# Index logits taken three per job from job 7 on, with seven top-k rounds and two low parts in other jobs, in a two-layer gated token-mixer trunk on Trainium2

## The chip, the core and the metric

The kernel runs on one core of one Trainium2 chip. The metric is the device time of one execution in microseconds (us).

## What is computed

A trunk of DEPTH = 2 layers on x of 512 tokens by 1024 channels, all in float32. Per layer, cut to what matters here:

```python
h = rms_norm(x, norm_g)
proj = h @ w_in       # a_u a_v a_z | q k v z_b | index queries, index key, head weights | g_a g_b
y_a = gelu(a_u) * spatial_gate(layer_norm(gelu(a_v))) * silu(a_z)
# sparse attention: the indexer picks the keys of every query
logits = einsum('bqhd,bsd->bqhs', qi, ki)                 # 8 index heads of 64
score  = einsum('bqh,bqhs->bqs', wi, relu(logits)) * idx_scale
idx    = top_k(where(admissible, score, -inf), 128)       # per query, shared by the 4 heads
y_b = attention(q, k[idx], v[idx]) * silu(b_z)
x = x + (sigmoid(g_a) * (y_a @ w_oa) + sigmoid(g_b) * (y_b @ w_ob)) @ w_out
```

## The kernel before

**Jobs.** TensorE (PE) works through 96 jobs per layer, numbered 0 to 95: four for the index queries (iq, 0 to 3), then k (4 to 7), q (8 to 11), v (12 to 25: v of branch B and v of branch A together), u (26 to 29), z_b (30 to 33), z_a (34 to 37), the gate g_a (38 to 51), w_oa (52 to 59), g_b (60 to 73), w_ob (74 to 81) and w_out (82 to 95). Each product runs in three passes, on a high and a low part of both operands. The groups of 14 jobs are seven half-size products with sums of blocks. A job of k, q, u, z_b or z_a is 24 matmuls of 512 columns, `three_pass`; a job of v or a gate is half of that.

**Engines.** Each engine has its own list of instructions, written out by one loop over the jobs. "Turn n" is what such a loop issues for job n. An engine takes its list strictly in order and waits at semaphores. In a turn VectorE (DVE) first makes low parts of weights (`remainder`, L1580, one 128 x 1024 subtraction per weight unit; which unit in which turn is in `quarters_in` and its tables, among them OB_UNITS); then it finishes the rope rotation of the job before (`rotated`, jobs 0 to 11); then layer norm, top-k rounds, and the job's own result (`evacuate`); last the side work (`beside`). Up to job 37 the rounds come before `evacuate`, from job 38 on after `beside`. ScalarE (ACT) makes the high parts of weights (L1181), copies results out of PSUM, and does the exponentials and the relu.

**Weights.** They come in units of 512 KB into a ring of four raw buffers (w_raw). The DMA of unit u waits for the low part of unit u-4 (s_wlo). Units of sums are added to the buffer's old content by a DMA that GpSimd (POOL, L763) issues. PE waits for the low part of a unit before the first job that uses it.

**Banks.** Results of k, q, u, z_b and z_a rotate through PSUM banks 0, 1, 2 (job number mod 3). The gate jobs take bank 0, 2, 1 or 6; job 38 takes bank 0, which job 36 had, and job 39 takes bank 1, which job 37 had. For z_a, `evacuate` on VectorE (L1791) multiplies ScalarE's tanh(z/2) plus 1 with z in the bank, and only then signals the bank free.

**Index logits.** IDX_STEPS are 24 steps: query blocks b = 1, 2, 3 (128 queries; a block sees 256, 384 or 512 keys), 8 heads each. Step i is two matmuls (L886, L887) into bank 3 + i % 2, a relu on ScalarE (L1427) into probs[i % 2], and a weighted add into score on VectorE (`index_add`, L1640 for the first head and L1642 for the others; after head 8 the mask, L1648). PE waits for relu i-2, relu i for add i-2. AFTER_IDX says after which job steps are taken: two after each of jobs 6 to 17.

**Top-k.** The 128 keys of a block are 16 rounds of MAX8 and MATCH_REPLACE8 (`topk_round`, L1653, L1654) over its whole score, and one closing pass (L1656). TOPK_SLOTS gives {job: [(block, rounds)]}.

**Attention.** 16 steps, block by block, of QK, row max (L1671), exponential (L1451), scaling (L1457), transposes on PE (L926), and the product with v (L917): step 0 after job 36, 1 after job 38, then after every second job; steps 8 to 11 (block 2) after jobs 52 to 58, 12 to 15 (block 3) from job 60 on. Transposes of step i are issued behind the next slot's job.

## Time and profile before

| | |
|---|---|
| median of 3 runs | 788.0 us (787.08 to 789.36) |
| the profiled execution | 789.16 us, span 786.5 us |
| mean granted TensorE clock | 0.998 of full |
| PE busy | 764.6 us (97%) |
| VectorE busy | 621.1 us (79%) |
| ScalarE busy | 447.1 us (57%) |

The profiled execution is 1.16 us above the median; 2.66 us of it lie outside the span. Layer 1 repeats layer 0 some 384 to 385 us later. PE's matmuls overlap, so that of a wait of PE the distance between starts counts: it is some 0.17 us more than the idle time that the rows show.

### The profile page before, as it was taken

The page shows a single profiled execution, that of the slowest core. Times are in us where ns is not written, and L with a number is a line of the kernel's source. Part 1 is how long each engine was busy: PE and PEld are TensorE (multiplying, and loading weights), DVE is VectorE, ACT ScalarE, POOL GpSimd, SP SyncE. Part 2 cuts the span into 40 slices and gives each one's busy share as a digit, 9 for nine tenths or more (in the row PEclk, how much of TensorE's full clock was granted, in tenths as well). Part 3 has the DMA queues.
Part 4 walks back from the last instruction along what each step waited for, and adds up shares of the span by engine and source line. Part 5 has one row for each costly group of instructions (what it writes and reads, how often), then busy time and mean ns, then how long its engine had stood idle before and what let it go on. Part 6 is the DMA issues. An engine that isn't in the chain of part 4 may idle for free.

```text
span 786.5 us, 12260 instructions
## 1 busy us (share of the span) xinstructions
PE 764.6 (97%) x4364; PEld 666.6 (85%) x4364; DVE 621.1 (79%) x1075; ACT 447.1 (57%) x834; POOL 153.3 (19%) x143
## 2 busy tenths in 40 slices
PE   7999999999999999999999999899999999999998
PEld 7988877888898879988899887688889987899886
DVE  5766899898878785779986679988988768756895
ACT  5588786341576437735665977564326763577242
POOL 1445430000130103012214453100012101110130
PEclk9999999999999999999999999999999999999999
DMA  9849998422695328685875888962348743486684
GB/s 333 274 94 201 188 196 260 137 77 70 195 169 183 73 63 142 206 237 105 194 232 156 180 164 173 266 212 81 107 75 215 167 135 53 94 151 223 176 144 125
DMA packets 60876, 128.34 MB, mean 163 GB/s; under 512 B 3984, under 2 KB 10320, under 8 KB 60816
## 3 DMA queue, kind: packets, MB, share of 16 engines
q0 software_dynamic: 26544, 55.66, 38.7%
q1 hardware_dynamic: 33984, 71.31, 27.6%
q8 instruction: 35, 0.57, 0.3%
q10 hardware_dynamic: 288, 0.59, 0.2%
q14 instruction: 25, 0.20, 0.1%
HBM read 107.63 MB, written 10.49 MB: 150 GB/s over the span
## 4 chain that ended last, share of the span: by engine, by line
PE 71%; DVE 14%; issue 7%; ACT 5%; DMA 3%; POOL 0%; DVEq 0%; ACTq 0%; POOLq 0%
PE bank L945 10%; PE bank L944 10%; PE bank L943 10%; PE bank L1012 6%; PE bank L1094 5%; PE bank L1014 5%; PE bank L1013 5%; DVE score L1654 2%; DVE w_lo L1580 2%; DVE top L1653 2%; PE bank L1041 2%; PE bank L980 2%; PE bank L1042 2%; PE bank L1043 2%; PE bank L982 2%
## 5 line engine op out<-in xcount | busy, mean ns | idle before, releaser
L1580 DVE TENSOR_TENSOR w_lo<-w_raw,w_hi 128x1024 fp32r<-128x1024 f32 x168 | 203.2, 1219 | 31.9 <-ACT w_hi L1181 27.6
L1181 ACT ACTIVATE w_hi<-w_raw 128x1024 fp32r<-128x1024 f32 x168 | 173.1, 1053 | 36.7 <-DMA w_raw<-in_w_out 14.7
L763 POOL DMA_DIRECT2D w_raw<-in_w_in x48 | 59.1, 1231 | 374.1 <-DVE w_lo L1580 374.1
L1012 PE MATMUL bank<-h_hi,w_lo 128*128 128x256 f32 x256 | 76.5, 299 | 3.5 <-DVEq L1761 3.5
L943 PE MATMUL bank<-h_lo,w_hi 128*128 128x512 f32 x192 | 75.2, 392 | 0.0
L945 PE MATMUL bank<-h_hi,w_hi 128*128 128x512 f32 x192 | 74.7, 389 | 0.0
L944 PE MATMUL bank<-h_hi,w_lo 128*128 128x512 f32 x192 | 74.7, 389 | 0.0
L1014 PE MATMUL bank<-h_hi,w_hi 128*128 128x256 f32 x256 | 73.2, 286 | 0.0
L1013 PE MATMUL bank<-h_lo,w_hi 128*128 128x256 f32 x256 | 73.1, 286 | 0.0
L1451 ACT ACTIVATE probs<-probs,neg_max,rstd 128x128 f32<-128x128 f32 (+3 forms) x32 | 20.9, 654 | 69.8 <-DVE neg_max L1675 69.7
L1653 DVE MAX8 top<-score 128x8 f32<-128x256 f32 (+2 forms) x96 | 53.5, 557 | 5.0 <-DVE g_a L1802 1.9
L1012 PE MATMUL bank<-hs,w_lo 128*128 128x256 f32 x192 | 56.3, 293 | 0.0
L1012 PEld LDWEIGHTS bank<-h_hi,w_lo 128*128 128x128 f32 x256 | 49.8, 195 | 5.5 <-DVEq L1761 3.9
L1014 PE MATMUL bank<-hs,w_hi 128*128 128x256 f32 x192 | 53.8, 280 | 0.0
L1013 PE MATMUL bank<-hs,w_hi 128*128 128x256 f32 x192 | 53.8, 280 | 0.0
L1654 DVE MATCH_REPLACE8 score<-top,score 128x256 f32<-128x256 f32 (+2 forms) x96 | 52.1, 543 | 0.0
L1013 PEld LDWEIGHTS bank<-h_lo,w_hi 128*128 128x128 f32 x256 | 49.7, 194 | 1.6 <-issue 1.4
L943 PE MATMUL bank<-w_lo,h_hi 128*128 128x512 f32 x128 | 50.4, 394 | 0.0
L945 PE MATMUL bank<-w_hi,h_hi 128*128 128x512 f32 x128 | 50.1, 391 | 0.0
L944 PE MATMUL bank<-w_hi,h_lo 128*128 128x512 f32 x128 | 49.9, 390 | 0.0
L1014 PEld LDWEIGHTS bank<-h_hi,w_hi 128*128 128x128 f32 x256 | 49.7, 194 | 0.0
L945 PEld LDWEIGHTS bank<-h_hi,w_hi 128*128 128x128 f32 x192 | 36.0, 188 | 7.5
(234 smaller groups left out, 1986.0 us busy)
## 6 DMA issues: line engine op xcount, KB each, us to landing
w_raw<-in_w_in SPq DMA_DIRECT2D x84, 512.0 KB, 4.6
w_raw<-in_w_in POOLq DMA_DIRECT2D x48, 512.0 KB, 6.1
w_raw<-in_w_out POOLq DMA_DIRECT2D x16, 512.0 KB, 6.6
w_raw<-in_w_out SPq DMA_DIRECT2D x12, 512.0 KB, 4.2
out<-x_sb POOLq DMA_DIRECT2D x4, 1024.0 KB, 5.8
w_raw<-in_w_oa SPq DMA_DIRECT2D x8, 512.0 KB, 3.4
w_raw<-in_w_ob SPq DMA_DIRECT2D x8, 512.0 KB, 4.4
x_sb<-out POOLq DMA_DIRECT2D x2, 2048.0 KB, 10.6
```

The costliest lines, as they stand in the source:

```text
L763: pool.dma_start(w_raw[:, slot], block_weights(layer, u), accum_op=ALU.add) \
L943: nc.tensor.matmul(dst, s_h, m_l, start=(n == 0), stop=False)
L944: nc.tensor.matmul(dst, s_l, m_h, start=False, stop=False)
L945: last = nc.tensor.matmul(dst, s_h, m_h, start=False, stop=(n == len(pairs) - 1))
L1012: nc.tensor.matmul(dst, w_lo[:, wk, col], a_hi[:, k], start=first and i == 0, stop=False, skip_group_check=True)
L1013: nc.tensor.matmul(dst, w_hi[:, wk, col], a_lo[:, k], start=False, stop=False, skip_group_check=True)
L1014: last = nc.tensor.matmul(dst, w_hi[:, wk, col], a_hi[:, k], start=False, stop=(k == HALF_K - 1), skip_group_check=True)
L1094: last = nc.tensor.matmul(dst[:, 0:width], h[:, k, tok], w[:, k, first:first + width], start=(k == 0 and n == 0), stop=(k == KD - 1 and n ...
L1181: nc.scalar.activation(hi, w_raw[:, raw_slot(layer, u)], ACT.Copy).then_inc(s_whi.sem, 1)
L1580: nc.vector.tensor_tensor(lo, w_raw[:, raw_slot(layer, u)], hi.bitcast(F32), ALU.subtract) \
L1653: vec.link(dve, nc.vector.max(top8[:], s))
L1654: vec.link(dve, nc.vector.match_replace(s, top8[:], s, TAKEN))
```

## The change

1. **Index logits.** Steps 0 and 1 stay behind job 6. For each of the jobs 7 to 11 there is now one step in the middle (MID_IDX: 2, 5, 8, 11, 14: PE issues it after the fourth of the eight k of the job) and two steps behind it (3, 4; 6, 7; 9, 10; 12, 13; 15, 16). Two each follow jobs 12, 13, 14 and one (23) job 15. ScalarE takes the relu of the middle step ahead of its `evacuate`, VectorE the add ahead of the rounds and of `evacuate`.
2. **Top-k rounds.** By job, as rounds before and after: 9: 0, 1; 10: 3, 2; 11: 3, 1; 27: 3, 4; 28: 3, 4; 31: 1, 2; 34: 0, 1; 35: 0, 1; 46: 1, 0; 47: 1, 0; 45: 1, 2; 49: 1, 0; 50: 0, 1; 55: 2, 1; 57: 1, 0; 58: 0, 1; 59: 1, 0. Job 37 has two rounds of block 3 where it had two of block 2, job 39 one of block 3 where it had one of block 2. Block 1 closes in turn 28 (27 before), block 2 in 35 (39), block 3 in 58 (59).
3. **Low parts.** In OB_UNITS VectorE's second unit of the next group is made in turn +11 where it was in +10: turns 23, 49 and 71 for 22, 48 and 70.

z keeps its tanh on ScalarE and its product on VectorE. The diff:

```diff
--- before.py
+++ after.py
@@ -110,7 +110,7 @@
 
 GATE_UNITS = dict(scalar=[0, 1, 3, 5], vector=[1, 2, 5, 7])
 LATE_GATE_UNITS = dict(scalar=[0, 0, 2, 2, 3, 4, 6, 7, 8, 8], vector=[0, 1, 2, 3, 4, 5, 7, 7, 8, 9])
-OB_UNITS = dict(scalar=[9, 9, 10, 11], vector=[10, 10, 11, 12])
+OB_UNITS = dict(scalar=[9, 9, 10, 11], vector=[10, 11, 11, 12])
 LATE_UNITS = dict(scalar=[-1, 0, 1, 1, 4, 5, 6, 7, 9, 9], vector=[-1, 1, 2, 3, 5, 6, 7, 8, 9, 10])
 
 
@@ -182,7 +182,10 @@
 AFTER_K = {JOB_K[t] + 2: t for t in range(TILES)}
 AFTER_Q = {JOB_Q[t] + 2: t for t in range(TILES)}
 IDX_STEPS = [(b, h) for b in range(1, TILES) for h in range(IH)]
-AFTER_IDX = {6 + n // 2: [n - n % 2, n - n % 2 + 1] for n in range(len(IDX_STEPS))}
+MID_IDX = {JOB_K[3] + i: 2 + 3 * i for i in range(5)}
+AFTER_IDX = {JOB_K[2]: [0, 1], **{n: [i + 1, i + 2] for n, i in MID_IDX.items()},
+             **{JOB_V[i]: [17 + 2 * i, 18 + 2 * i] for i in range(3)}, JOB_V[3]: [23]}
+assert sorted([*MID_IDX.values(), *(i for steps in AFTER_IDX.values() for i in steps)]) == list(range(len(IDX_STEPS)))
 AFTER_WS = JOB_V[8]
 LN_TILES = {JOB_ZB[0]: [0, 1], JOB_ZB[1]: [2, 3]}
 AFTER_MIX = {JOB_ZB[3]: [0, 1], JOB_ZA[0]: [2, 3]}
@@ -206,10 +209,10 @@
 
 VA_DONE = {JOB_V[9]: 0, JOB_V[10]: 1, JOB_V[11]: 2, JOB_V[12]: 3}
 
-TOPK_SLOTS = {10: [(1, 3)], 11: [(1, 3)], 19: [(1, 1)], 20: [(1, 1)], 21: [(1, 1)], 26: [(1, 4)], 27: [(1, 3)],
-              28: [(2, 3)], 29: [(2, 4)], 30: [(2, 1)], 31: [(2, 1)], 32: [(2, 2)], 33: [(2, 2)], 37: [(2, 2)], 39: [(2, 1)],
-              **{n: [(3, 1)] for n in range(41, 53, 2)}, 46: [(3, 1)], 52: [(3, 1)], 53: [(3, 2)],
-              54: [(3, 1)], 55: [(3, 2)], 56: [(3, 1)], 57: [(3, 1)], 59: [(3, 1)]}
+TOPK_SLOTS = {9: [(1, 1)], 10: [(1, 2)], 11: [(1, 1)], 19: [(1, 1)], 20: [(1, 1)], 21: [(1, 1)], 26: [(1, 4)], 27: [(1, 4)],
+              28: [(1, 1), (2, 3)], 29: [(2, 4)], 30: [(2, 1)], **{n: [(2, 2)] for n in range(31, 34)}, 34: [(2, 1)], 35: [(2, 1)],
+              37: [(3, 2)], 39: [(3, 1)], 41: [(3, 1)], 43: [(3, 1)], 45: [(3, 2)], 50: [(3, 1)], 51: [(3, 1)], 52: [(3, 1)],
+              53: [(3, 2)], 54: [(3, 1)], 55: [(3, 1)], 56: [(3, 1)], 58: [(3, 1)]}
 
 
 
@@ -1078,6 +1081,8 @@
                     def ready(k):
                         if j == 0 and k % 2 == 0:
                             pe.wait_ge(s_wlo.sem, s_wlo.at(layer, UNIT_FIRST[g] + k // 2 + 1))
+                        if k == HALF_K and n in MID_IDX:
+                            index_logits(layer, MID_IDX[n])
                 last = three_pass(dst[:], pairs, ready)
                 last.then_inc(s_job.sem, 1)
 
@@ -1415,16 +1420,19 @@
                         act_.join(act)
                         act.sem_inc(s_rotc.sem, 1)
 
+            def index_relu(layer, i):
+                b, h = IDX_STEPS[i]
+                w = P * (b + 1)
+                act.wait_ge(s_idxp.sem, s_idxp.at(layer, i + 1))
+
+                if i >= 2:
+                    act.wait_ge(s_idx.sem, s_idx.at(layer, i - 1))
+                nc.scalar.activation(probs[:, i % 2, 0:w], bank[3 + i % 2][:, 0:w], ACT.Relu).then_inc(s_relu.sem, 1)
+
             def beside(layer, n):
 
                 for i in AFTER_IDX.get(n, []):
-                    b, h = IDX_STEPS[i]
-                    w = P * (b + 1)
-                    act.wait_ge(s_idxp.sem, s_idxp.at(layer, i + 1))
-
-                    if i >= 2:
-                        act.wait_ge(s_idx.sem, s_idx.at(layer, i - 1))
-                    nc.scalar.activation(probs[:, i % 2, 0:w], bank[3 + i % 2][:, 0:w], ACT.Relu).then_inc(s_relu.sem, 1)
+                    index_relu(layer, i)
                 if n == AFTER_WS:
                     act.wait_ge(s_wst.sem, s_wst.at(layer, 1))
                     four = bank[5][:].rearrange("p (c q) -> p c q", c=A_GROUPS)
@@ -1535,6 +1543,8 @@
                         rounded(layer, u)
                     if AFTER_QI.get(n) == 0:
                         rotated_copied(layer, n)
+                    if n in MID_IDX:
+                        index_relu(layer, MID_IDX[n])
                     evacuate(layer, n)
                     if AFTER_QI.get(n) != 0:
                         rotated_copied(layer, n)
@@ -1975,6 +1985,8 @@
                             small_remainder(layer + 1)
                             remainder(layer + 1, 2)
                     layer_norm(layer, n)
+                    if n in MID_IDX:
+                        index_add(layer, MID_IDX[n])
                     if n < JOB_GA[0]:
                         topk(n)
                     evacuate(layer, n)
```

The three places where the order on VectorE decides. First, turn 11 behind its rotation, and turn 12 up to its own (the last q job and the first v job; rot is the rotated q that PE transposes). Before:

```order
L1653 MAX top<-score 128x8
L1654 MATCH_REPLACE score<-top,score 128x256
L1653 MAX top<-score 128x8
L1654 MATCH_REPLACE score<-top,score 128x256
L1653 MAX top<-score 128x8
L1654 MATCH_REPLACE score<-top,score 128x256
L1778 RECIPROCAL rstd<-std 128x4
L1642 SCALAR_TENSOR_TENSOR score<-probs,head_w,score 128x384 x2
L1580 TENSOR_TENSOR w_lo<-w_raw,w_hi 128x1024
L1590 SCALAR_TENSOR_TENSOR rope_b<-stage,rope_g 128x4x64
L1591 TENSOR_TENSOR rope_b<-stage,rope_g 128x4x64
L1594 TENSOR_TENSOR rot<-rope_a,rope_b 128x512
```

and now:

```order
L1652 SCALAR_TENSOR_TENSOR score<-probs,head_w,score 128x384
L1663 MAX top<-score 128x8
L1664 MATCH_REPLACE score<-top,score 128x256
L1788 RECIPROCAL rstd<-std 128x4
L1652 SCALAR_TENSOR_TENSOR score<-probs,head_w,score 128x384
L1658 TENSOR_TENSOR score<-score,diag 128x128
L1650 TENSOR_SCALAR score<-probs,head_w 128x512
L1590 TENSOR_TENSOR w_lo<-w_raw,w_hi 128x1024
L1600 SCALAR_TENSOR_TENSOR rope_b<-stage,rope_g 128x4x64
L1601 TENSOR_TENSOR rope_b<-stage,rope_g 128x4x64
L1604 TENSOR_TENSOR rot<-rope_a,rope_b 128x512
```

Two of the three rounds are gone. In place of two adds of 384 columns stand two of 384, a mask and a first add of 512 columns; the low part and the rotation of turn 12 follow as before.

Second, turn 37 (the last z_a job; the first row belongs to attention step 0 in turn 36, the last is the product that frees bank 1 for job 39). Before:

```order
L1661 RECIPROCAL row_inv<-row_sum 128x1
L1653 MAX top<-score 128x8
L1654 MATCH_REPLACE score<-top,score 128x384
L1653 MAX top<-score 128x8
L1654 MATCH_REPLACE score<-top,score 128x384
L1791 SCALAR_TENSOR_TENSOR silu_um<-t_half,bank 128x512
```

and now:

```order
L1671 RECIPROCAL row_inv<-row_sum 128x1
L1663 MAX top<-score 128x8
L1664 MATCH_REPLACE score<-top,score 128x512
L1663 MAX top<-score 128x8
L1664 MATCH_REPLACE score<-top,score 128x512
L1801 SCALAR_TENSOR_TENSOR silu_um<-t_half,bank 128x512
```

The two rounds ahead of the product run over 512 columns where they ran over 384. Two turns earlier, in turn 35, a round and the closing pass of block 2 now stand ahead of that turn's product, and in turn 34 a round.

Third, turns 46 (from its last attention row on), 47 and 48 (g_a; of the rows with g_a<-g_a,bank the last one is the add that PE's job 50 waits for). Before:

```order
L1661 RECIPROCAL row_inv<-row_sum 128x1
L1653 MAX top<-score 128x8
L1654 MATCH_REPLACE score<-top,score 128x512
L1580 TENSOR_TENSOR w_lo<-w_raw,w_hi 128x1024
L1760 TENSOR_TENSOR g_a<-g_a,bank 128x2x256
L1653 MAX top<-score 128x8
L1654 MATCH_REPLACE score<-top,score 128x512
L1580 TENSOR_TENSOR w_lo<-w_raw,w_hi 128x1024 x2
L1760 TENSOR_TENSOR g_a<-g_a,bank 128x2x256
```

and now:

```order
L1671 RECIPROCAL row_inv<-row_sum 128x1
L1590 TENSOR_TENSOR w_lo<-w_raw,w_hi 128x1024
L1770 TENSOR_TENSOR g_a<-g_a,bank 128x2x256
L1590 TENSOR_TENSOR w_lo<-w_raw,w_hi 128x1024
L1770 TENSOR_TENSOR g_a<-g_a,bank 128x2x256
```

The rounds of turns 46 and 47 and one of two low parts are gone from ahead of turn 48's add. One round was put into turn 45.

## Rows read from the trace of the kernel before

**Rows 1.** The page: busy time; shares of the chain that ended last.

```profile
PE 764.6 (97%) x4364; PEld 666.6 (85%) x4364; DVE 621.1 (79%) x1075; ACT 447.1 (57%) x834; POOL 153.3 (19%) x143
...
PE 71%; DVE 14%; issue 7%; ACT 5%; DMA 3%; POOL 0%; DVEq 0%; ACTq 0%; POOLq 0%
```

**Rows 2.** Waits of PE, layer 0, 57 to 130 us: total, times, longest.

```profile
PE bank L1041 <- DVE w_lo L1580: 1.3, 1, 1.3
PE bank L872 <- DVE rot L1594: 1.2, 1, 1.2
```

**Rows 3.** The same view, layer 1, 441 to 516 us.

```profile
PE bank L886 <- ACT probs L1427: 0.8, 1, 0.8
```

**Rows 4.** The same view, layer 0, 240 to 300 us.

```profile
PE bank L926 <- ACT probs L1457: 1.4, 2, 1.0
```

**Rows 5.** VectorE by form: count, busy us, mean ns, idle before.

```profile
L1653 DVE MAX8 top<-score 128x8 f32<-128x512 f32 x32 | 22.0, 688 | 3.3 <-DVE g_a L1802 1.9 <-DVE g_a L1760 0.9
L1654 DVE MATCH_REPLACE8 score<-top,score 128x512 f32<-128x512 f32 x32 | 21.6, 676 | 0.0
...
L1653 DVE MAX8 top<-score 128x8 f32<-128x384 f32 x32 | 17.8, 557 | 1.1 <-DVE z_b L1784 0.5
L1654 DVE MATCH_REPLACE8 score<-top,score 128x384 f32<-128x384 f32 x32 | 17.4, 543 | 0.0
L1653 DVE MAX8 top<-score 128x8 f32<-128x256 f32 x32 | 13.6, 425 | 0.6
...
L1642 DVE SCALAR_TENSOR_TENSOR score<-probs,head_w,score 128x512 f32<-128x512 f32 x14 | 10.5, 751 | 1.9 <-ACT probs L1427 1.0 <-DVE v_b L1735 0.5
...
L1654 DVE MATCH_VALUE_LOAD score<-top,score 128x8 f32 x96 | 8.8, 92 | 3.3
L1642 DVE SCALAR_TENSOR_TENSOR score<-probs,head_w,score 128x384 f32<-128x384 f32 x14 | 8.6, 613 | 0.3
...
L1656 DVE TENSOR_SCALAR score<-score 128x384 f32<-128x384 f32 x2 | 0.7, 361 | 0.1
```

**Rows 6.** PE in order of time: index steps 8 and 9, to job 11.

```profile
83.68 0.42 PE L886 MATMUL bank<-ki_lo,qi_t 128*128 128x384 f32 x1
...
84.47 0.39 PE L943 MATMUL bank<-w_lo,h_hi 128*128 128x512 f32 x1
```

**Rows 7.** VectorE in order of time, turns 11 and 17: start, us.

```profile
90.65 0.43 DVE L1590 SCALAR_TENSOR_TENSOR rope_b<-stage,rope_g 128x256 f32<-128x256 f32 x1 [0.89 <-PE bank L872]
...
116.94 1.22 DVE L1580 TENSOR_TENSOR w_lo<-w_raw,w_hi 128x1024 fp32r<-128x1024 f32 x1
```

**Rows 8.** The same view, turns 28, 30, 36 and 37.

```profile
152.84 2.36 DVE L1580 TENSOR_TENSOR w_lo<-w_raw,w_hi 128x1024 fp32r<-128x1024 f32 x2 [1.06 <-ACT w_hi L1181]
...
165.31 0.18 DVE L1847 RECIPROCAL ln_rstd<-ln_std 128x4 f32<-128x4 f32 x1 [0.22 <-ACT ln_std L1209]
...
204.00 0.69 DVE L1791 SCALAR_TENSOR_TENSOR silu_um<-t_half,bank 128x512 f32<-128x512 f32 x1 [0.70 <-ACT t_half L1380]
...
207.63 0.16 DVE L1661 RECIPROCAL row_inv<-row_sum 128x1 f32<-128x1 f32 x1 [0.70 <-ACTq L1455]
...
210.19 0.69 DVE L1791 SCALAR_TENSOR_TENSOR silu_um<-t_half,bank 128x512 f32<-128x512 f32 x1
```

**Rows 9.** PE in order of time: the first matmul of job 39.

```profile
212.01 0.36 PE L1012 MATMUL bank<-h_hi,w_lo 128*128 128x256 f32 x1
```

**Rows 10.** PE in order of time, layer 0: the first matmul of job 50.

```profile
249.48 0.39 PE L1012 MATMUL bank<-h_hi,w_lo 128*128 128x256 f32 x1 [1.73 <-DVEq L1761]
```

**Rows 11.** The same in layer 1: job 50.

```profile
634.32 0.39 PE L1012 MATMUL bank<-h_hi,w_lo 128*128 128x256 f32 x1 [1.74 <-DVEq L1761]
```

**Rows 12.** A window behind it: busy times, then granted clock, DMA share, GB/s.

```profile
634.60:638.10 3.50, 3.50 (x19) 3.50 (x19) 2.51 (x7) 2.64 (x6) 0.00 (x0) 0.51 0.71 248
```

**Rows 13.** PE in order of time: scores of attention step 8, layers 0 and 1.

```profile
259.84 0.49 PE L935 MATMUL bank<-k_t,q_t 128*128 128x384 f32 x1
...
646.15 0.49 PE L935 MATMUL bank<-k_t,q_t 128*128 128x384 f32 x1
```

## Prediction

> **What bounds the kernel now.** I read the page first: PE is busy for 97% of the span, and the chain that ended last runs over PE for 71% and over VectorE for 14% [rows 1]. So there is no second bound of any length, only places where PE waits, and a gain has to be one of these waits. The views of PE's waits give them. In the v stage of layer 0 PE waits twice: 1.2 us for the rotation of the last q tile, 1.3 us for a weight low part [rows 2]. Layer 1 adds 0.8 us in which an index matmul waits for a relu [rows 3]. In the g_a stage job 50 waits 1.73 us for VectorE's add of turn 48 [rows 10]; in the w_oa and g_b stages two transposes of probabilities wait 1.4 us in all [rows 4]. Every one goes back to VectorE being late. With the tails of the matmuls (0.17 us per wait) the two later groups cost 1.9 and 1.7 us in each layer. The question for each part is therefore what VectorE has to do before a given instruction, and whether PE stands waiting for it.
>
> There is a second loss in layer 1. After the same wait as in layer 0 [rows 10, 11] the granted clock falls to 0.51 for 3.5 us [rows 12], that is, to 1.2 GHz of 2.4. Between job 50's first matmul and the scores of attention step 8, layer 0 takes 259.84 - 249.48 = 10.36 us, layer 1 takes 646.15 - 634.32 = 11.83 us [rows 10, 11, 13]: the fall cost 1.5 us.
>
> **Prices.** A top-k round is MAX8, the load and MATCH_REPLACE8: 0.688 + 0.092 + 0.676 = 1.46 us over 512 columns, 0.557 + 0.092 + 0.543 = 1.19 over 384, and about 0.425 + 0.092 + 0.41 = 0.93 over 256 (the replace taken as long as the MAX8, as in the other widths). An index add is 0.75 us (512) or 0.61 (384), a closing pass 0.36 (384) [rows 5]. On PE two steps of 384 columns take 84.47 - 83.68 = 0.79 us, 0.4 each [rows 6].
>
> **Index logits and the v stage.** No step is added, so PE's own time stays. Five more steps (10 to 14, 384 columns) are issued before job 11 ends: PE is 5 x 0.4 = 2.0 us later there, and VectorE's turn 11, which waits for the transposes behind job 11 (the 0.89 us ahead of it [rows 7]), starts 2.0 us later. From there to the low part at 116.94 VectorE works without a pause. In this stretch two rounds of 256 are gone (-1.9), four adds of 384 (-2.5) make room for two of 512 (+1.5) and a mask (0.3 us, taken like the closing pass): -2.6. Net the low part that PE waits for comes 0.6 us earlier. The wait for the rotation vanishes, but its 1.2 us come back as a longer wait at that low part. Layer 1 has the same 0.6 and the relu's 0.8, because no relu stands behind a late weight any more. Together **-2.0 us**. It could be nothing (VectorE late by what it gained), or all the waits of rows 2 and 3 with their tails, 6.7 us for both layers.
>
> The middle steps are new waits: PE's step i stands in mid job, with all the job's matmuls queued behind it, and needs relu i-2. ScalarE comes to that relu only behind its squares, root and copies for the job before, PE to mid job behind four transposes, two steps and twelve matmuls: by the two lists about a tie for jobs 7 and 9, and room for the others. No row shows such a wait; the nearest are 0 and the 0.8 of rows 3. I take 0.15 us per layer, nearest to the tie, **+0.3**.
>
> **Rounds into z_b and z_a.** This is the part that costs. In turn 28 VectorE starts at 152.84 behind an idle 1.06 us, waiting for a high part that ScalarE can make only behind job 27 [rows 8]; that idle time swallows turn 27's extra round. From there to the product of turn 37 at 210.19 there is added: one round of 256 (0.93) and the closing pass of block 1 (0.3), rounds of 384 in turns 31, 34 and 35 (3.57), the closing pass of block 2 (0.36), and in turn 37 two rounds of 1.46 for two of 1.19 (0.54): 5.7, with the few hundredths between instructions 5.8 us. The waits that this can fill are 0.22 us (turn 30) and 0.70 us (turn 36, tanh of job 36). The other 0.70, the exponential of attention step 0, is a round trip that stays [rows 8]. So the product that frees bank 1 ends 4.9 us later, at 215.8 instead of 210.88. PE began job 39, which needs that bank, at 212.01 [rows 9], 0.1 us of which is the signal's way: 1.0 us of slack. PE waits **3.9 us in each layer, +7.8**, in which the late scaling of step 0's probabilities (4 us later too) is contained. VectorE then stays 1 us behind PE until turn 44, so that banks 2 and 6 come back just in time; I count nothing, at most 0.5 us per layer.
>
> **Rounds out of g_a and w_oa, the low part.** Ahead of the add of turn 48 two rounds leave (turns 46 and 47), one arrives (turn 45), and one low part leaves: -1.46 - 1.22 = -2.7 us, more than the wait of 1.9. It goes in both layers: **-3.8**. The moved low part falls into turn 49, ahead of the add for job 51, but behind a turn that starts 2.7 us earlier: hidden; without that cover it would cost its 1.2. In turns 22 and 70 nothing waits: 0. For the transposes behind job 58 PE needs step 10's maximum (turn 56): by then two rounds in all are gone (-2.9), while PE comes 1.9 earlier; so 1.0 us of the first wait (the longest, 1.0 plus its tail [rows 4]) goes. By step 11 it is a third round, and the second wait goes whole. **-3.3** for both layers. The DMAs hang on the low parts: in z_a they start up to 5 us later, but the high parts made from them are a group away.
>
> **Sum** without the clock: -2.0 + 0.3 + 7.8 - 3.8 - 3.3 = -1.0 us. **The clock.** Waits of 1.73 us were followed by a fall once in two layers [rows 10 to 12]. Now these waits are gone (-1.5), but a wait of 3 us and one of half a microsecond stand around job 38 in each layer, longer than the one that brought the fall. I take a fall in both layers: 3.4 us at half clock, +1.7 each, +3.4. Total 789.16 - 1.0 - 1.5 + 3.4 = 790.1 us for the profiled execution; the median of the runs lies 1.16 us below that execution, which gives **788.9 us**.
>
> **Rivals.**
> 1. *The clock stays full behind the new wait.* For it: in layer 0 the 1.73 us did not bring a fall. Against it: layer 1, and the new wait is twice as long. 785.5 us. The Trainium skill (TensorE: Matmul & The Clock Gate, "HAM oscillation") lets only idle gaps longer than these waits, and than the one forecast here, cost the clock; by that rule this rival would be the forecast, but this trace shows a fall behind 1.74 us of idle time, so it does not agree. Chance 0.16.
> 2. *VectorE takes the rounds in its stride in z_b and z_a*, because its 79% leave room and the waits there are longer than I read. Then +7.8 and +3.4 fall away: 777.7 us. Against it: between 152.84 and 210.19 only 0.92 us of idle time can be filled. Chance 0.10.
> 3. *Slower: the clock also falls in the v stage.* PE now reaches job 18 without an earlier wait and meets a VectorE that is late with two low parts in succession: the 2.8 us that rows 2 give with their tails, less the 0.6 gained, are 2.2 us of waiting with six matmuls between. If such a pair brings the clock down, which a single 1.3 did not, both layers pay 1.7 us more: 792.3 us. [...] Chance 0.26.
>
> **Numbers.** The forecast has 0.48. 0.3% is 2.4 us, about what a measurement of this kernel can tell from no change: below 785.6 is faster, above 790.4 slower. Faster is rival 2, more than half of rival 1 and a little of the forecast: 0.24. Slower is rival 3: 0.26. Same: 0.50. The range runs from 784.9 (rival 1 and a v stage that gains a little more) to 792.6 (rival 3 with the 0.5 us of the banks) and leaves rival 2 out.
>
> **What would show it.** Right: in the view of PE's waits job 39 waits 3 to 4 us for the signal behind VectorE's silu_um product, in both layers; the wait before job 50 and those of the transposes behind jobs 58 and 60 are gone; the wait for the rotation is gone, two for w_lo in job 18 remain; the granted clock falls behind job 39's wait. Wrong: no wait at job 39 (then rival 2), or waits in mid job at L886's successor of more than 0.5 us, which would mean that the relus are late and that the v stage starts later than I think.

## The result and the profile after

| | before | after |
|---|---|---|
| median, range | 787.58 us (787.08 to 789.36, 4 runs) | 797.8 us (795.81 to 799.12, 4 runs) |
| profiled execution | 789.16 us, span 786.5 us | 797.21 us, span 794.6 us |
| mean granted clock | 0.998 | 0.994 |

The ratio is 1.0114, with a 95% interval of 1.0093 to 1.0134: the change makes the kernel 10 us **slower**. I had forecast 788.9 us, no change, in a range up to 792.6. The profiled executions differ by 8.05 us, the medians by 10.2, because before the median lies 1.6 us under the profiled execution (1.16 by the three runs that the forecast knew) and after the change 0.6 us above it.

The page of the changed kernel, busy times and the chain that ended last, which answers to [rows 1]:

```profile
PE 768.6 (97%) x4364; PEld 669.1 (84%) x4364; DVE 618.9 (78%) x1075; ACT 448.7 (56%) x834; POOL 154.0 (19%) x143
...
PE 57%; DVE 25%; ACT 7%; issue 6%; DMA 5%; DVEq 0%; ACTq 0%; SPq 0%
```

VectorE does no more than before, yet its share of the chain has grown from 14 to 25%, and that of the DMA from 3 to 5%. (Lines from L886 of before are 3 to 10 higher now: L1580 is L1590, L1012 is L1015, L1760 is L1770, L1041 is L1044.)

Waits of PE after the change (total, times, longest), layer 0 in four stretches: 57 to 130, 130 to 146, 204 to 265, 265 to 300 us. They answer to [rows 2, 4]:

```profile
PE bank L1044 <- DVEq L1748: 1.4, 1, 1.4
PE bank L1044 <- DVE w_lo L1590: 0.3, 1, 0.3
PE bank L875 <- DVEq L1642: 0.3, 1, 0.3
PE bank L889 <- ACT probs L1430: 0.2, 1, 0.2
...
PE bank L1044 <- DVEq L1746: 3.4, 2, 2.5
...
PE bank L1015 <- DVEq L1803: 2.7, 1, 2.7
PE bank L1015 <- DVEq L1771: 0.8, 1, 0.8
PE bank L929 <- ACT probs L1465: 0.3, 1, 0.3
...
PE bank L920 <- DVE z_b L1890: 0.2, 1, 0.2
```

The wait for the rotation is gone, and so is the old wait before job 50. In job 18 0.3 us are left of the wait for the low part; 1.4 us stand in job 17 now, for a bank that the add of turn 15 frees. So VectorE's lateness comes back one job earlier than forecast, and at another instruction. Two waits are new and large: 3.4 us for the adds of turns 22 and 23 (2.5 in job 24 and 0.9 in job 25, where before PE lost 0.3 us at most), and 2.7 us in job 39. A third, 0.8 us, is in job 51.

To place each microsecond I took the end of each job's last matmul from the trace, and from it how long each group of jobs takes. In us, layer 0 / layer 1, against the terms of the prediction for both layers:

| jobs | before | after | difference, both | predicted |
|---|---|---|---|---|
| start to 23 | 134.14 / 120.70 | 133.32 / 119.56 | -2.0 | -2.0 + 0.3 |
| 24, 25 | 5.76 / 5.44 | 9.45 / 7.93 | **+6.2** | 0 |
| 26 to 37 | 69.15 / 69.15 | 69.15 / 69.15 | 0 | 0 |
| 38, 39 | 6.08 / 6.07 | 11.08 / 12.16 | +11.1 | +7.8 + 3.4 |
| 40 to 49 | 32.62 / 32.62 | 32.54 / 32.39 | -0.3 | 0 |
| 50 | 4.87 / 6.36 | 2.88 / 2.88 | -5.5 | -3.8 - 1.5 |
| 51 | 3.97 / 3.96 | 5.04 / 5.04 | **+2.2** | 0 |
| 52 to 61 | 37.79 / 37.81 | 36.37 / 36.03 | -3.2 | -3.3 |
| 62 to 95 | 104.21 / 102.67 | 103.83 / 102.67 | -0.4 | 0 |

The rows for which I had worked out a term are right to 0.3 us. The two set to nothing are 8.3 us; against the sum of 790.1 the profiled execution is 7.1 us longer, the other rows together being 1.2 us better than forecast.

**Job 39.** PE in order of time, layer 0, with the idle time ahead in brackets:

```profile
214.71 0.28 PE L1017 MATMUL bank<-h_hi,w_hi 128*128 128x256 f32 x1
215.34 0.33 PE L929 MATMUL bank<-eye,probs 128*128 128x128 f32 x1 [0.34 <-ACT probs L1465]
215.50 0.39 PE L938 MATMUL bank<-k_t,q_t 128*128 128x128 f32 x2
218.58 0.39 PE L1015 MATMUL bank<-h_hi,w_lo 128*128 128x256 f32 x1 [2.69 <-DVEq L1803]
```

VectorE in the same time:

```profile
214.76 0.68 DVE L1663 MAX8 top<-score 128x8 f32<-128x512 f32 x1
...
217.07 0.68 DVE L1664 MATCH_REPLACE8 score<-top,score 128x512 f32<-128x512 f32 x1
217.78 0.69 DVE L1801 SCALAR_TENSOR_TENSOR silu_um<-t_half,bank 128x512 f32<-128x512 f32 x1
```

The two rounds of turn 37 run from 214.76 to 217.75, and the product that frees bank 1 starts behind them. The clock falls to half in both layers: in layer 0 1.35 us after the wait has ended, in layer 1 already within it (job 39's first matmul starts at 606.96 there), and for 6.8 us (two windows; columns as in [rows 12]):

```profile
219.90:223.40 3.50, 3.50 (x19) 3.50 (x18) 2.77 (x8) 1.04 (x5) 1.20 (x1) 0.51 0.79 294
605.60:612.50 6.90, 5.54 (x26) 5.54 (x27) 5.74 (x11) 3.24 (x9) 1.20 (x1) 0.51 0.55 170
```

Here an idle time of 2.69 us, with 0.34 us shortly ahead, cost the clock in both layers, as 1.74 us did once in [rows 11, 12]. The Trainium skill (TensorE: Matmul & The Clock Gate, "HAM oscillation") has only longer idle gaps than this cost the clock; this trace does not agree.

The same wait need not bring a fall. In experiment 6, layer 1, job 39 waits as long and the clock stays full:

```profile
635.18 0.39 PE L1015 MATMUL bank<-h_hi,w_lo 128*128 128x256 f32 x1 [2.69 <-DVEq L1803]
...
633.00:640.00 7.00, 4.82 (x40) 4.83 (x41) 5.80 (x13) 3.71 (x8) 1.20 (x1) 1.00 0.63 223
```

Jobs 38 and 39 take 9.80 us there, 3.7 more than before the change: that is the wait alone. What the changed kernel takes beyond it, 1.3 us in layer 0 and 2.4 us in layer 1, is the clock.

**Jobs 24 and 25.** ScalarE in order of time, after the change:

```profile
125.30 1.06 ACT L1186 ACTIVATE w_hi<-w_raw 128x1024 fp32r<-128x1024 f32 x1 [2.86 <-DMA w_raw<-in_w_in]
129.29 1.06 ACT L1186 ACTIVATE w_hi<-w_raw 128x1024 fp32r<-128x1024 f32 x1 [2.93 <-DMA w_raw<-in_w_in]
130.37 1.28 ACT L1282 ACT_TABLE_LOAD   x1
...
132.83 2.00 ACT L1186 ACTIVATE w_hi<-w_raw 128x1024 fp32r<-128x1024 f32 x2 [0.17 <-ACT ws_t L1440]
```

and VectorE:

```profile
133.92 1.23 DVE L1590 TENSOR_TENSOR w_lo<-w_raw,w_hi 128x1024 fp32r<-128x1024 f32 x1 [0.73 <-ACT w_hi L1186]
135.06 0.68 DVE L1745 TENSOR_TENSOR v_a<-v_a,bank 128x512 f32<-128x512 f32 x1
...
136.72 2.33 DVE L1590 TENSOR_TENSOR w_lo<-w_raw,w_hi 128x1024 fp32r<-128x1024 f32 x2
138.96 0.68 DVE L1745 TENSOR_TENSOR v_a<-v_a,bank 128x512 f32<-128x512 f32 x1
```

Read it backwards. Job 24 waits for the add at 135.06; that stands behind a low part, that behind a high part at 132.83, that behind the table load and two copies, and these behind the high part at 129.29, which waited for **the last weight transfer of v to land**. Before the change the same high part ran at 126.37:

```profile
126.37 1.06 ACT L1181 ACTIVATE w_hi<-w_raw 128x1024 fp32r<-128x1024 f32 x1 [2.12 <-DMA w_raw<-in_w_in]
```

So ScalarE waited for landings in the v stage before the change too; the prediction does not read that view. The transfer itself (tile w_raw, POOL's queue, the last v transfer: issued at 118.5 us before, at 117.6 after), first before, then after:

```profile
DMA to landing us min/median/max: 7.9/7.9/7.9
```

```profile
DMA to landing us min/median/max: 11.7/11.7/11.7
```

It starts 0.9 us earlier and lands 2.9 us later. What it shares the DMA engines with has moved. SyncE's first two weight transfers of the next group, u, start at 119.97 and 122.12 us (122.36 and 123.49 before), because the low parts that give back their buffers come earlier. The v transfer ahead of it is issued 2.2 us earlier than it, where it was 4.0 us. And SyncE's two copies of hs (the high and the low part of a sum of blocks of h, 512 KB each, written to the DRAM buffer `hold`) run beside it for 3.9 and 6.7 us, before for 3.8 and 5.0. SyncE's queue after the change, 119.5 to 122.5 us:

```profile
L688 SPq DMA_DIRECT2D w_raw<-in_w_in x2: 384/384/384, 120.0 to 122.1; - x2
...
DMA to landing us min/median/max: 8.1/8.2/8.3
```

Two windows of each kernel (busy times, granted clock, DMA share, GB/s) show DMA engines that were never free, before as after (in a share above 1 the packets of an engine overlap); first before, then after:

```profile
116.00:120.00 4.00, 2.65 (x12) 1.85 (x11) 3.90 (x6) 2.12 (x5) 1.21 (x1) 1.00 1.11 216
120.00:124.00 4.00, 4.00 (x19) 3.23 (x18) 3.97 (x6) 2.75 (x4) 0.00 (x0) 1.00 1.05 302
```

```profile
116.00:120.00 4.00, 3.73 (x16) 2.71 (x15) 3.74 (x4) 3.52 (x6) 1.85 (x2) 1.00 1.10 268
120.00:124.00 4.00, 4.00 (x19) 3.22 (x18) 2.05 (x4) 1.43 (x2) 0.00 (x0) 1.00 1.10 271
```

From job 11's end to job 23's end PE became 3.0 us faster in layer 0 (44.03 to 41.05) and 3.8 us in layer 1; from job 11's end to the last v landing it is 36.2 and 36.7 us before, 37.0 and 35.4 after. So in layer 0 the stream of weights came later, in layer 1 earlier but by less than PE did. PE ran ahead of its weights and gave the lead back in jobs 24 and 25. That was the theory to test.

### The profile page after: what moved, and what is told of

Same layout as the page of the kernel before. It is cut to its first block, busy times and chain, and to the rows that moved or that the text cites. A ratio compares the mean times of both kernels' runs of the same rounds, so it can differ in the third digit from the quotient of the medians.

```text
span 794.6 us, 12256 instructions
## 1 busy us (share of the span) xinstructions
PE 768.6 (97%) x4364; PEld 669.1 (84%) x4364; DVE 618.9 (78%) x1075; ACT 448.7 (56%) x834; POOL 154.0 (19%) x143
## 4 chain that ended last, share of the span: by engine, by line
PE 57%; DVE 25%; ACT 7%; issue 6%; DMA 5%; DVEq 0%; ACTq 0%; SPq 0%
PE bank L948 7%; PE bank L947 7%; PE bank L946 7%; DVE w_lo L1590 6%; PE bank L1015 5%; PE bank L1016 5%; PE bank L1017 5%; PE bank L1099 4%; DVE score L1664 4%; DMA w_raw<-in_w_in 4%; DVE top L1663 4%; PE bank L983 3%; PE bank L984 3%; PE bank L985 3%; ACT w_hi L1186 2%
## 5 line engine op out<-in xcount | busy, mean ns | idle before, releaser
L1590 DVE TENSOR_TENSOR w_lo<-w_raw,w_hi 128x1024 fp32r<-128x1024 f32 x168 | 203.4, 1220 | 42.3 <-ACT w_hi L1186 36.8
L1015 PE MATMUL bank<-h_hi,w_lo 128*128 128x256 f32 x256 | 77.6, 303 | 7.0 <-DVEq L1803 5.4
L1015 PEld LDWEIGHTS bank<-h_hi,w_lo 128*128 128x128 f32 x256 | 50.9, 199 | 10.4 <-DVEq L1803 6.5
L1015 PE MATMUL bank<-hs,w_lo 128*128 128x256 f32 x192 | 56.1, 292 | 0.0
```

The source lines that it names most:

```text
L1015: nc.tensor.matmul(dst, w_lo[:, wk, col], a_hi[:, k], start=first and i == 0, stop=False, skip_group_check=True)
L1590: nc.vector.tensor_tensor(lo, w_raw[:, raw_slot(layer, u)], hi.bitcast(F32), ALU.subtract) \
```

## The experiments

Ratios are to runs of the kernel before on the same chip, whose median was 789.58 us for the first four, 790.5 for the next four, 790.28 for the ninth to twelfth and 788.84 for the last; for the change the ratio is 1.0114. A ratio is not the quotient of the two medians and can differ from it by 0.15%. Times of jobs are those of the profiled execution, one for each kernel.

**1. Index part alone.** The tables TOPK_SLOTS and OB_UNITS as before, the rest as in the change.

```diff
-OB_UNITS = dict(scalar=[9, 9, 10, 11], vector=[10, 11, 11, 12])
+OB_UNITS = dict(scalar=[9, 9, 10, 11], vector=[10, 10, 11, 12])
...
-TOPK_SLOTS = {9: [(1, 1)], 10: [(1, 2)], 11: [(1, 1)], 19: [(1, 1)], 20: [(1, 1)], 21: [(1, 1)], 26: [(1, 4)], 27: [(1, 4)],
+TOPK_SLOTS = {10: [(1, 3)], 11: [(1, 3)], 19: [(1, 1)], 20: [(1, 1)], 21: [(1, 1)], 26: [(1, 4)], 27: [(1, 3)],
...
```

> The index logits go three per job as in the change; all top-k rounds and the two low parts are where they were before. Theory A: the loss in the v stage belongs to the index part alone. The change's products end 3.1 us later than before at the end of job 25 in layer 0 and 1.4 us in layer 1, out of waits of 2.7 and 1.0 us (layer 0) and 1.2 and 1.0 us (layer 1) before jobs 24 and 25; they stay, and job 39's wait and the clock falls behind it are not there, while the old wait before job 50 is. That gives about 787.6 + 4.5 = 792. Rival B: those waits come from the rounds that went from jobs 10 and 11 to 9 and 27, the index part gains the 2 us that I predicted: 785.6.

794.79 us, ratio 1.006 (1.0038 to 1.0083), 5.2 us above before: A. Waits of PE, layer 0, 99 to 140 us:

```profile
PE bank L875 <- DVE rot L1604: 2.0, 1, 2.0
PE bank L1044 <- DVEq L1746: 1.7, 1, 1.7
PE bank L1044 <- DVEq L1748: 1.4, 1, 1.4
PE bank L1044 <- DVE w_lo L1590: 0.3, 1, 0.3
```

Job 24 waits; job 25 does not (2.79 us). With all six rounds in turns 10 and 11 the rotation is awaited 2.0 us where it was 1.2, so that the wait vanishes in the change only by the two rounds that leave: jobs 14 to 18 take 20.90 us here and 18.60 in the change. Jobs 38 and 39 are as before (6.07 us). By jobs, the index part alone has lost 2.2 us by the end of job 23 (both layers together), and 3.8 us more in job 24.

**2. Rounds of blocks 2 and 3 back.**

```diff
-              28: [(1, 1), (2, 3)], 29: [(2, 4)], 30: [(2, 1)], **{n: [(2, 2)] for n in range(31, 34)}, 34: [(2, 1)], 35: [(2, 1)],
-              37: [(3, 2)], 39: [(3, 1)], 41: [(3, 1)], 43: [(3, 1)], 45: [(3, 2)], 50: [(3, 1)], 51: [(3, 1)], 52: [(3, 1)],
-              53: [(3, 2)], 54: [(3, 1)], 55: [(3, 1)], 56: [(3, 1)], 58: [(3, 1)]}
+              28: [(1, 1), (2, 3)], 29: [(2, 4)], 30: [(2, 1)], 31: [(2, 1)], 32: [(2, 2)], 33: [(2, 2)], 37: [(2, 2)], 39: [(2, 1)],
+              **{n: [(3, 1)] for n in range(41, 53, 2)}, 46: [(3, 1)], 52: [(3, 1)], 53: [(3, 2)],
+              54: [(3, 1)], 55: [(3, 2)], 56: [(3, 1)], 57: [(3, 1)], 59: [(3, 1)]}
```

> The change with the rounds of blocks 2 and 3 (jobs 28 to 59) back where they were before; the index part, block 1's rounds and the low parts as in the change. Theory A: TensorE's 2.85 us wait in job 39 goes in both layers, and the clock falls behind it too (11.1 us in all), but the waits in job 50 (1.9 us a layer, with the clock's fall in layer 1) and before the transposes after jobs 58 and 60 come back (6.5 us in all): 797.8 - 11.1 + 6.5 = 793.2. Rival B: the wait in job 39 comes of everything in that layer standing later behind the v stage, not of the rounds: it stays, and the time is above 797.8.

790.8 us, ratio 1.0009 (0.9997 to 1.0021): A in kind, and 4 us better than I expected: 2 us are this chip's own time of the kernel before, the rest for the most part the clock, which stays full behind jobs 50 and 51. Job 39 takes 3.20 us in both layers, as before the change. Jobs 50 and 51 take 3.74 + 4.75 us instead of 4.87 + 3.97: the low part in turn 49 shifts part of the wait from job 50 to 51.

**3. Turn 37's rounds into turns 43 and 49.**

```diff
-              37: [(3, 2)], 39: [(3, 1)], 41: [(3, 1)], 43: [(3, 1)], 45: [(3, 2)], 50: [(3, 1)], 51: [(3, 1)], 52: [(3, 1)],
+              39: [(3, 1)], 41: [(3, 1)], 43: [(3, 2)], 45: [(3, 2)], 49: [(3, 1)], 50: [(3, 1)], 51: [(3, 1)], 52: [(3, 1)],
```

> The change with the two rounds of block 3 in VectorE's turn 37 put into turns 43 and 49. Theory A: they stand 2.98 us ahead of the product of job 37 that gives bank 1 back to job 39, so TensorE's 2.85 us wait there goes, and with it the clock falls at 219.9 and 605.6 us: 11.1 us less, given back at most 1 us by the two rounds' new places, so 787 (786 to 789). Rival B: the product is late for another reason (the rounds in turns 34 and 35, ScalarE's tanh): job 39 still waits 1 to 3 us in each layer, and the time stays above 791.

794.3 us, ratio 1.0063 (1.0041 to 1.0085): my number is wrong by 7, by 5 against its before. PE in order of time, job 39 and job 44 in layer 0, then VectorE's product of turn 37:

```profile
215.75 0.39 PE L1015 MATMUL bank<-h_hi,w_lo 128*128 128x256 f32 x1 [0.71 <-DVEq L1803]
...
233.81 0.39 PE L1015 MATMUL bank<-hs,w_lo 128*128 128x256 f32 x1 [0.71 <-DVE w_lo L1590]
...
214.94 0.69 DVE L1801 SCALAR_TENSOR_TENSOR silu_um<-t_half,bank 128x512 f32<-128x512 f32 x1 [0.95 <-ACT t_half L1385]
```

The clock stays full in both layers, and jobs 38 and 39 take 7.8 us instead of 11.1 and 12.2: 7.6 us are back. But 0.7 us of the wait stays although turn 37 has no round at all. VectorE has nothing to do ahead of that product: it stands idle for 0.95 us until ScalarE's tanh of job 37, which is issued behind the exponential and the scaling of attention step 0, and these waited for VectorE's row maximum. So what moved into turns 28 to 35 (four rounds and closing passes) makes that chain late enough for a wait, and the two rounds of turn 37 had hidden the chain's last 0.95 us. And the two rounds cost 5.2 us in their new places, not 1: jobs 40 to 49 are 1.0 and 1.5 us longer, job 51 0.3 in each layer, jobs 57 to 61 1.0 in each.

**4. u's weights only behind v's last landing.**

```diff
                         sp.wait_ge(s_wlo.sem, s_wlo.at(layer, u - RAW + 1))
+                    if u == UNIT_FIRST[V_G + 1]:
+                        sp.wait_ge(*landed(layer, u - 1))
                     slot = raw_slot(layer, u)
```

> The change, and SyncE's queue starts the first weight transfer of u only when the last added transfer of v has landed. Theory A: in the change the two u transfers start at 119.97 and 122.12 us (before: 122.36 and 123.49) because the low parts come earlier, share the DMA engines with the last two transfers of v, and make the last one land at 129.27 instead of 126.35; VectorE's add of job 22 follows from that landing, and job 24 waits for it. Held back, the last v transfer lands near 127 in layer 0, the waits before jobs 24 and 25 lose 2 to 3.7 us in layer 0 and 1 to 2.5 in layer 1: 793 (791.6 to 794.8). Rival B: the transfers of v are late by themselves (later starts at 103 us and a full DMA), the landing stays near 129 and the u weights come later yet: 797.8 or more.

794.57 us, ratio 1.006 (1.004 to 1.008): A. It is 5.0 us above its before, where the change is 10.2 above; between the two profiles it is 3.2 us. The same transfer as above, issued at 117.8 us:

```profile
DMA to landing us min/median/max: 9.3/9.3/9.3
```

It lands at 127.1 us (11.7 and 10.1 us for the transfer in the two layers of the change, 9.3 and 8.8 here). Job 24 takes 3.33 and 3.08 us instead of 5.56 and 4.03, job 25 an unchanged 3.90. So a second thing makes job 25 wait.

**5. The low parts back.**

```diff
-OB_UNITS = dict(scalar=[9, 9, 10, 11], vector=[10, 11, 11, 12])
+OB_UNITS = dict(scalar=[9, 9, 10, 11], vector=[10, 10, 11, 12])
```

> The change with the two low parts back in VectorE's turns 22 and 48 (and 70); index logits and rounds as in the change. Theory A: the low part that now stands in turn 23 ahead of the add of turn 23 is what job 25 waits for (1.03 us with its tail in each layer), and the one in turn 49 is what job 51 waits for (0.97 us). Both waits go; ahead of the adds of turns 22 and 48 it costs less, since in turn 22 VectorE sits idle for a high part anyway and in turn 48 there is 1.0 us of slack: -2.3 us in the v stage of both layers together, -2.1 us in job 51, +0.5 us in job 50, so 794. Rival B: it is the same work one turn earlier, and the waits only move to jobs 24 and 50, at their full 1.2 us: 797.5 to 798.

800.16 us, ratio 1.011 (1.0073 to 1.0147): against A, and no better than the change. Jobs 25 and 51 do lose their waits (3.07 and 2.75; 3.97 us), and job 50 pays 0.5 us in each layer, as expected. But in turn 22 the low part costs more than it saves: job 24 waits 3.9 us, and 2.6 in layer 1,

```profile
PE bank L1044 <- DVEq L1746: 3.9, 1, 3.9
```

and the clock falls with that in both layers, here in layer 0:

```profile
136.80:143.60 6.80, 6.10 (x14) 4.84 (x15) 5.95 (x10) 2.58 (x6) 0.00 (x0) 0.50 0.77 233
```

Job 24 takes 9.40 and 7.20 us. That is rival B for job 24. Inside the changed kernel the moved low part was a relief of turn 22, paid for in turn 23.

**6. The third index step behind the job.**

```diff
-MID_IDX = {JOB_K[3] + i: 2 + 3 * i for i in range(5)}
-AFTER_IDX = {JOB_K[2]: [0, 1], **{n: [i + 1, i + 2] for n, i in MID_IDX.items()},
+MID_IDX = {}
+AFTER_IDX = {JOB_K[2]: [0, 1], **{JOB_K[3] + i: [2 + 3 * i, 3 + 3 * i, 4 + 3 * i] for i in range(5)},
```

> The change with the third index step of jobs 7 to 11 behind the job, with the two others, instead of in mid job. Theory A: the third step then needs the relu of the first, which ScalarE does only behind the copy of the job's result, so that TensorE waits about 0.8 us at each of five places in each layer: 806. Rival B: TensorE has room there, since VectorE sets the pace of the v stage, and a wait in jobs 7 to 11 only takes the place of the 1.5 us wait in job 18: 798 to 800.

825.66 us, ratio 1.0449 (1.0411 to 1.0488). A, but three times my price: the five waits are 1.9 to 2.6 us each where I took 0.8, and the clock falls four times among them. PE's waits, layer 0, 57 to 150 us:

```profile
PE bank L889 <- ACT probs L1430: 11.8, 5, 2.6
```

A relu behind the job comes only after ScalarE's squares, root and copies for that job (64.76 to 66.80 us for the first of the five). The middle step is what makes three per job possible: in the change it costs PE 0.2 and 0.4 us of waiting in the two layers.

**7. The second and fourth together, v's low part back in turn 22.** The v group alone gets its own table, used for g == V_G:

```diff
+V_UNITS = dict(scalar=[9, 9, 10, 11], vector=[10, 10, 11, 12])
```

> The kernel of the second experiment (rounds of blocks 2 and 3 back), with the wait of the fourth experiment (u's first weight transfer only when v's last has landed), and in the v stage alone the low part back in turn 22. Theory A: the waits before jobs 24 and 25 go almost whole (jobs 24 and 25 took 8.95 us in layer 0 and 7.96 in layer 1 in the second experiment, 5.76 and 5.44 before): 790.8 - 5.7 = 785.1, faster than before. Rival B: with the low part back in turn 22, the add of turn 22 is late again by its 1.2 us in each layer, or the later u weights make job 26 wait: 787.5 to 789.

789.74 us, ratio 0.9991 (0.9973 to 1.0009): B. Job 24 takes 5.21 and 4.51 us, job 25 2.72 and 2.77. With u's weights held back, the high parts for the two low parts in turn 22 are late: ScalarE waits for their landings and makes them at 131.29 and 132.63 us, VectorE's two low parts take from 132.39 to 134.95, and the add that job 24 waits for stands behind them.

**8. The fourth's wait in the kernel before.**

> The kernel before, with nothing but the wait of the fourth experiment: u's first weight transfer only when v's last has landed. Theory A: before the change the last v transfer landed in time and jobs 24 and 25 hardly waited (0.28 us in layer 0), so the wait gives nothing: within 0.5 us of before. Rival B: the wait helps by itself, whatever the index logits do, and the fourth experiment says nothing about the change: 1.5 us or more below before.

789.86 us, ratio 0.9992 (0.9975 to 1.0009): A. In its profile the wait even costs job 24 1.1 and 0.6 us. The last v transfer gains nothing there by having u's out of its way (8.7 and 8.0 us, 7.9 and 7.5 in the kernel before). The traffic of u was no loss before; the index part made it one.

**9. One low part a turn further.**

```diff
-OB_UNITS = dict(scalar=[9, 9, 10, 11], vector=[10, 11, 11, 12])
+OB_UNITS = dict(scalar=[9, 9, 10, 11], vector=[10, 11, 12, 12])
```

> The change with one low part of each group moved one VectorE turn further: from turn 23 to 24, 49 to 50 and 71 to 72 (vector=[10, 11, 12, 12]). Theory A: job 25 waits for the add of turn 23, which stands behind two low parts; behind one it comes 1.2 us earlier, and so for job 51 and turn 49. Both waits go in both layers: 1.13 + 1.18 + 1.07 + 1.08 = 4.5 us less than the change, so 5.7 us above before instead of 10.2. Rival B: the low part is only passed on: job 26 or the transposes of the attention step behind job 50 wait for it, and the time stays within 1.5 us of the change.

794.71 us, ratio 1.0071 (1.0046 to 1.0095), 4.4 us above before by the medians and 5.6 by the ratio: A by the time. Job 25 takes 2.72 and 2.79 us, job 51 3.97: both waits are gone. But jobs 57 to 61 take 0.55 us more in each layer than in the change, where a product of attention waits: half of what job 51 gains is lost there again. In layer 0 its job 24 waits longer than in the change and the clock falls with it (7.43 us instead of 5.56).

**10. All three together.** The rounds of the second, the wait of the fourth, the low parts of the ninth; their diffs, one on the other.

> The second experiment (rounds of blocks 2 and 3 where they were before) with the wait of the fourth and the low parts of the ninth. Theory A: from job 11's end to job 25's the v stage is set by the stream of its weights. With u's transfers held back it ran in 48.2 and 48.0 us (before: 49.8 and 50.3, the change 50.5 and 49.0), with job 25's wait of 1.0 us still in it; without that 47.2 and 47.0. Against the second experiment that is 2.7 + 2.2 us, and 1.6 us in job 51: its 1.2 us above before become 5.3 us below before. Rival B: the three do not add up, because held back u weights are late for the low part in turn 22: at most 2 us below before.

785.45 us, ratio 0.9944 (0.9924 to 0.9965): 4.8 us below its before, A. PE's waits, layer 0, 120 to 260 us:

```profile
PE bank L1046 <- DVEq L1748: 1.2, 1, 1.2
PE bank L1017 <- DVEq L1773: 0.6, 1, 0.6
```

**11. SyncE's two copies of hs to `hold` kept back too.**

```diff
+                    if u == UNIT_FIRST[V_G + 1]:
+                        sp.wait_ge(*landed(layer, u - 1))
                     if u in (UNIT_FIRST[V_G] + 8, UNIT_FIRST[V_G + 1]):
```

> The tenth kernel, and the two copies of hs to hold are held back as well until v's last weight transfer has landed. Theory A: the last two v transfers share the DMA engines with these two copies (they start 24 us behind job 11's end, in the same 10 us); without them the last one lands at about 32 us behind job 11's end instead of 34.6 (fourth experiment), and what is left of job 24's wait (0.5 us in layer 0) goes: 0.5 to 1 us below the tenth kernel. Rival B: the copies cost the v transfers nothing: landing and time as in the tenth.

785.29 us, ratio 0.9943 (0.9926 to 0.9961). The last v transfer now takes

```profile
DMA to landing us min/median/max: 6.5/6.5/6.5
```

against 11.7, 31.8 us behind job 11's end, and job 24 does not wait (3.00 and 2.89 us). That is A's mechanism; the medians of 10 and 11 can't be told apart, their spans are 783.6 and 781.6 us. By jobs, from the second experiment to this one, the held back transfers give 3.3 us (jobs 12 to 24) and the later low part some 2.9 (jobs 25 and 51, less what jobs 52 to 61 give back). The copies were not held back with the change's own rounds.

**12. One round from turn 55 forward.**

```diff
-              28: [(1, 1), (2, 3)], 29: [(2, 4)], 30: [(2, 1)], 31: [(2, 1)], 32: [(2, 2)], 33: [(2, 2)], 37: [(2, 2)], 39: [(2, 1)],
+              28: [(1, 1), (2, 3)], 29: [(2, 4)], 30: [(2, 1)], 31: [(2, 2)], 32: [(2, 2)], 33: [(2, 2)], 37: [(2, 2)], 39: [(3, 1)],
...
-              54: [(3, 1)], 55: [(3, 2)], 56: [(3, 1)], 57: [(3, 1)], 59: [(3, 1)]}
+              54: [(3, 1)], 55: [(3, 1)], 56: [(3, 1)], 57: [(3, 1)], 59: [(3, 1)]}
```

> The tenth kernel with one round taken out of turn 55: a round of block 2 goes from turn 39 to turn 31, one of block 3 from 55 to 39. Theory A: the transposes behind jobs 58 and 60 lose their waits of 1.13 and 0.6 us in each layer (3.4 us); turn 37's product is 1.2 us later against 1.0 us of slack, at most 0.3 us a layer: 2.8 us below the tenth kernel. Rival B: the slack before job 39 is used up and PE waits a full microsecond there, with banks coming late behind it: less than 1.5 us below the tenth.

784.92 us, ratio 0.9944 (0.9926 to 0.9962): B. Against the tenth, jobs 57 to 61 are 1.5 and 1.9 us shorter, but job 39 is 0.7 us longer in each layer and jobs 40 to 49 0.8, where a low part comes late. Even one round more ahead of turn 37 is too many.

**13. The eleventh without the index part** and without block 1's moved rounds: the tables and the order of before, with the eleventh's wait and the ninth's low parts.

> The kernel before, with the held back copies and u weights and the later low parts of the eleventh kernel, but without three index steps per job and without the moved rounds of block 1. Theory A: the index part is worth its 2 us only where the stream of v's weights is no longer in the way; without it the rotation's wait behind job 13, the wait of job 18 and the relu's in layer 1 come back, and only job 50 gains: jobs 12 to 25 take some 49.5 us from job 11's end instead of 46.7, the whole is 2 us below before (788.3 where before is 790.3), 3 us above the eleventh kernel. Rival B: the whole gain of the tenth and eleventh kernels is that of the held back transfers and the low parts, the index logits play no part: within 1 us of the eleventh kernel, 5 us below before.

786.15 us, ratio 0.9967 (0.9953 to 0.9981), between A and B by the time. The rotation's 1.2 and the low part's 1.4 us are back,

```profile
PE bank L1043 <- DVE w_lo L1582: 1.4, 1, 1.4
PE bank L874 <- DVE rot L1596: 1.2, 1, 1.2
```

and jobs 7 to 25 take 82.1 and 83.0 us instead of 81.8 and 82.0 in the eleventh: 1.4 us for the index part by the profiles, 0.24% (1.9 us) by the ratios, whose intervals overlap. More than half of the gain of the eleventh kernel stays without the index part. By jobs it is the low part's: job 50 takes 3.74 us in both layers where it took 4.87 and 6.36 (1.5 us of that the fall of the clock), while jobs 12 to 25 take 49.5 and 50.4 us, where they took 49.8 and 50.3. So the held back transfers show no gain without the index part, as experiment 8 says of u's alone. The low part without them was not run.

## Why the prediction was wrong

Two steps failed. The sum put jobs 24 and 25 at nothing, behind a v stage that it followed to job 18 only, and it put the moved low parts at nothing. These rows took 6.2 and 2.2 us more.

**"Index logits and the v stage": the -2.0 is right up to job 23 and wrong as an end.** The step followed PE and VectorE to the low part in job 18 and stopped there, as if nothing behind it had a limit of its own. The jobs to 23 did come 2.0 us earlier (predicted -1.7), though what is left of PE's waiting for VectorE stands for the most part in job 17 and not at the low part in job 18. Then the stream of v's weights set the end: +3.9 us in job 24. (The other 2.3 of the +6.2 us are job 25's, the next paragraph.) Experiments 1, 4, 8 and 11 show it: the wait in job 24 comes with the index part alone, it shrinks when u's transfers are held back and goes when the copies are too, and holding u's back does nothing in the kernel before. The DMA share, above 1 from 104 to 128 us, is so before the change too; what changed is what runs beside the last transfer, and when PE wants its result. My bound "it could be nothing" for this term was the wrong end: a gain upstream of a full transfer queue can turn into a loss, since it also starts the next group's transfers earlier beside the urgent ones. The same 512 KB transfer took 7.9 us before, 11.7 in the change, 9.3 and 6.5 in experiments 4 and 11. The Trainium skill (DMA: Bandwidth & Descriptors, "Rules for kernel authors") has transfers of SP and GpSimd run on the same 16 engines and interleave, so that spreading them brings no bandwidth; the trace agrees with that sharing. I had said of the DMAs only that they start later in z_a; that part held, jobs 26 to 37 did not move by 0.01 us.

**"In turns 22 and 70 nothing waits: 0" and "hidden; without that cover it would cost its 1.2".** Job 25 waits for the add of turn 23, which now stands behind two low parts: 1.0 us in each layer, and experiment 9 removes it by moving one of them. But against leaving them in turn 22 this is no loss (experiment 5). In turn 49 the cover was not there. Counted from job 49's end VectorE did finish turn 48 2.7 us earlier, but PE, without its wait in job 50, reaches job 51 2.0 us earlier itself. The prediction counts that for the transposes, and not here. The 0.7 us that are left went, with 0.3 more, into waiting for ScalarE's exponential, 1.76 us where it was 0.81 before:

```profile
257.21 0.16 DVE L1671 RECIPROCAL row_inv<-row_sum 128x1 f32<-128x1 f32 x1 [1.76 <-ACTq L1463]
257.29 2.34 DVE L1590 TENSOR_TENSOR w_lo<-w_raw,w_hi 128x1024 fp32r<-128x1024 f32 x2
259.55 0.68 DVE L1770 TENSOR_TENSOR g_a<-g_a,bank 128x512 f32<-128x512 f32 x1
```

Job 51 pays 1.07 us in each layer, near the 1.2 that I had named as the price without cover.

**Rounds into z_b and z_a: right.** Predicted 3.9 us of waiting in each layer and 1.7 for the clock; measured 2.7 of idle time in job 39 and 0.3 for the transpose ahead of it (3.7 from start to start), and 1.3 and 2.4 for the clock. The wait was 0.2 us over-sized in each layer, the fall in layer 1 twice as long as taken, and the errors cancel: that 11.1 came out for 11.2 is luck in part, and so is that the clock fell in both layers, which experiment 6's layer 1 shows it need not. Experiment 3 shows the mechanism, and that what moved into turns 28 to 35 is enough to cause a wait, through step 0's exponential and the tanh. The prediction had that chain only as "a round trip that stays". The 0.5 us for banks coming back late did not appear.

**Middle steps, rounds out of g_a and w_oa, clock.** Middle steps: 0.2 us of waiting in layer 0 and 0.4 in layer 1 (predicted 0.15 each), and worth keeping (experiment 6). Job 50: -5.5 for -5.3. Transposes: -3.2 for -3.3. Of the signs that I had named, the fall of the clock in both layers came; the "3 to 4 us" in the view of PE's waits read 2.7, and of the wait for w_lo in job 18 only 0.3 us remained.

**Rivals.** None was what happened. The third had the place almost right (the v stage, PE ahead of VectorE), but not the mechanism: the clock does not fall there in the change, with 2.54 us of idle time; it does in experiment 9 with 2.83,

```profile
136.13 0.79 PE L1044 MATMUL bank<-w_lo,h_hi 128*128 128x512 f32 x1 [2.83 <-DVEq L1746]
```

and in experiment 5 with 3.9 and, in layer 1, 2.6. The case I lacked is "the next resource is the transfer", which one view, ScalarE's waits for landings, would have offered.

## What to carry to other kernels

When a change makes a stage faster, follow the stage to its end in every resource that feeds it: open the waits of the engine that first touches landed data, and if it waits for transfers anywhere in the stage while the DMA share is at 1, the gain can stop there. Earlier free buffers start the next group's transfers, which slow the urgent ones on the same engines; a wait on the less urgent queue can give the gain back (3.3 us here by jobs 12 to 24; together with one low part in a later turn it turned 1.0009 into 0.9943). It is worth nothing where nobody waits for the urgent transfer (experiments 8 and 13). And a lead won on one engine is no cover by itself: take off what the engine that waits for it has gained too, and look for the next wait on the row of the leading engine, before calling moved work hidden.
